# Attention loop of a two-block network: scores transposed two steps after they are made instead of one, three score buffers instead of two, and a new order of the first block's small work

## The chip, the cores and the metric

The kernel is one program on 1 core of a Trainium2 chip. The metric is device time in microseconds (us) of one execution: the median of the runs before is 1471.96 us, over 3 runs from 1471.56 to 1475.67 us.

## What is computed

The network has two blocks on 512 tokens of width 1024. Only the first block's attention is touched. It has 16 query heads of 64 columns, eight of kind A and eight of kind B. Cut to what matters:

```
o_a   = banded_gqa(qa, ka, v_a, window 128, bias, sinks)
o_cmp = softmax over 31 compressed keys            (kind B)
o_sel = softmax over the selected keys             (kind B)
o_win = banded_gqa(qb, k_win, v_win, window 512)   (kind B)
o_b   = sigmoid(g0)*o_cmp + sigmoid(g1)*o_sel + sigmoid(g2)*o_win
y     = concat(o_a * silu(z_a), o_b * silu(z_b)) @ w_out
```

With 512 tokens the 16 selected blocks of 64 cover everything, so the selected branch is full causal attention, as the window branch is.

## The kernel before, in words

**Stages.** The program runs in one stream of stages: projections of the first block, its attention, the output projection, then the second block (convolution, retention, feed-forward). Outside attention nearly all time is weight matmuls of 512 columns, each weight tile converted into a rounded high part by ACT (L444) and a low part by DVE (L449).

**The attention loop.** It is software-pipelined by hand. There are 96 steps, one for each of 4 blocks of 128 queries, 3 branches (0 is A, 1 selected, 2 window) and 8 heads. `Step` (L122) decodes the step: 8 steps make a group, 3 groups make a query block `i`. A step's width is 128 keys times its number of key blocks: one for all groups of block 0; `i + 1` in branches 1 and 2; at most two in branch 0. So steps 0 to 23 are one block wide, 24 to 55 two, 56 to 71 three, 72 to 79 two, 80 to 95 four. Every engine has its own loop over the same step number `s`, and engines meet through semaphores:

- PE (L2096): at step `s` it makes the scores of step `s` in PSUM bank 1 or 0 (two matmuls, L2112 and L2113), then the product of probabilities and values of step `s - 3` (L2129), then the transposes of the exponentials of step `s - 1` into PSUM bank 2 or 3 (issued at L2138, recorded under the helper's line L1818). The scores of `s` wait until DVE has read those of `s - 2`; a transpose waits for that step's exponential; a product waits for that step's transposed copy.
- DVE (L1424): at step `s` it adds bias and mask to the scores and takes their row minimum in one instruction (L1437, from PSUM to `sc[:, s % 2]`), after the transposes of step `s - 2` have released that buffer. Then, if `s - 1` is even, it copies the transposed exponentials of step `s - 1` from PSUM (L1451) to `pt[:, 0]`. The parts of a finished group follow two, three and four steps into the next one: reciprocal of the sums (L1467), combination with the coefficient (L1480), and for the last group an addition.
- ACT (L989): at step `s` it takes the exponential in place with the row sum (L999), and copies the transposed exponentials of `s - 1` if that is odd (L1008).
- POOL adds a finished branch into `ob` (L777) and makes remainders of rounded keys (L753).

**The tail of a query block.** `tails_at` (L144) says at which step PE transposes `oa` and `ob` of block `i` (four transposes each) and DVE multiplies them by the gates `z` (L1493); ACT rounds the result one step later (L1019), POOL makes the remainder (L764). Before: steps `24 i + 29` and `24 i + 30`, for the last block 85 and 101.

**Small work of the first block.** Before the loop DVE turns gate logits into gates (L1408, L1410) and into the compressed branch's coefficients (L1413). `compressed_out(i)` on PE (L2064) makes the compressed output of block `i` with four matmuls at steps `CO_PE_AT = (0, 2, 4, 7)`, and DVE scales it into `ob` (L1420) at `CO_AT = (1, 4, 6, 9)`. ACT rounds the window branch's keys in four pieces (`k_round(2, ...)`, L926) at `K_WINDOW_AT = (3, 4, 5, 6)`; POOL takes the remainder of each (L753), and PE waits for them at step 16. At steps 61 and 63 ACT and DVE also convert weight tiles of the next stage.

**Order.** Each engine works its queue strictly in order, so an instruction that waits holds all behind it on that engine. PE's own order at a step, in the source:

```
pe.wait_ge(m["s_bias"], s - 1)                                   # scores of s - 2 read
pe.matmul(scores, q, k_high...); pe.matmul(scores, q, k_low...)  # step s
if s in CO_PE_AT: compressed_out(...)
t = s - 3: wait pt_a / pt_d; matmuls with the values             # product
t = s - 1: wait s_exp;       transposes                          # into bank 2 + t % 2
```

Of the kernel before, what the change touches and what calls it, by code (L numbers as in the profile page):

```python
# [27 lines left out]
ACT = mybir.ActivationFunctionType  # L28
# [63 lines left out]
CONVERT_AT = 61  # L92
CO_PE_AT = (0, 2, 4, 7)
CO_AT = (1, 4, 6, 9)
K_WINDOW_AT = (3, 4, 5, 6)

# [20 lines left out]
N_ATT = 8 * N_GROUPS  # L117
STEPS = N_ATT + 9
TAIL_LAST = N_ATT + 5

# [23 lines left out]
def tails_at(s):  # L144

    return [(i, half) for i in range(NI) for half in range(2)
            if s == (24 * i + 29 + half if i < NI - 1 else 24 * i + 13 + 16 * half)]

# [35 lines left out]
def hybrid_block(nc, x, c, w_ada, b_ada, norm_gain, w_in, b_nsa_gate, q_gain_a, k_gain_a, sinks,  # L184
# [8 lines left out]
    with ExitStack() as stack:  # L193
# [97 lines left out]

        sc = sb("scores_sb", [P, 2, S], R + 24)
        pt = sb("probs_t", [P, 2, S], R + 28)
        ob = sb("out_b", [P, NI, S], R + 32)
# [92 lines left out]
        def in_slot(t, slot, half):  # L387
# [7 lines left out]
        k_low = ((proj_r[:, KC], proj_r[:, VC]), [in_slot(wlo, KS_SLOT, g) for g in range(2)],  # L395
                 [in_slot(wlo, KW_SLOT, g) for g in range(2)])

        def two(ap):
# [241 lines left out]
        def _(pool):  # L640
# [193 lines left out]
        def _(act):  # L834
# [154 lines left out]
            for s in range(STEPS):  # L989
# [3 lines left out]
                if s < N_ATT:  # L993
                    G, n = divmod(s, 8)
                    act.wait_ge(m["s_bias"], s + 1)
                    if n == 0 and G >= 2:
                        act.wait_ge(m["comb_done"], G - 1)
                    w = att(s).width
                    a.activation(sc[:, s % 2, 0:w], sc[:, s % 2, 0:w], ACT.Exp, scale=-1.0,  # L999
                                 bias=row_min[:, G % 2, n:n + 1],  # L1000
                                 accum_out=den[:, G % 2, att(s).head:att(s).head + 1]).then_inc(m["s_exp"], 1)
                t = s - 1
                if 0 <= t < N_ATT and t % 2 == 1:
# [176 lines left out]
        def _(dve):  # L1180
# [225 lines left out]
            v.tensor_copy(cpt[:, 1], ps[:, 3]).then_inc(m["cpt_ev"], 1)  # L1406
            dve.wait_ge(m["gb_done"], 1)
            own(v.tensor_scalar(gates[:], gates[:], 1.0, None, ALU.add))  # L1408
            own.wait()
            own(v.reciprocal(gates[:], gates[:]))  # L1410
            own.wait()
            for g in range(2):
                own(v.tensor_tensor(ccoef[:, :, 4 * g:4 * g + 4], cden[:, g].rearrange("p (i j) -> p i j", i=NI),  # L1413
                                    gate_of(0)[:, :, 4 * g:4 * g + 4], ALU.mult))
            own.wait()

# [7 lines left out]
            for s in range(STEPS):  # L1424
                if s < N_ATT:
                    u = att(s)
                    G = s // 8
                    dve.wait_ge(m["s_mm"], s + 1)
                    if s >= 2:
                        dve.wait_ge(m["t_mm"], s - 1)  # L1430
                    if s == 56:
                        dve.wait_ge(m["kl_done"], 11)
                    if u.branch == 0:
                        band, start = band_a[:, u.head, 256 - u.width:256], nsink[:, u.head:u.head + 1]
                    else:
                        band, start = band_b[:, u.head, S - u.width:S], 3e38
                    v.tensor_tensor_reduce(sc[:, s % 2, 0:u.width], ps[:, 1 - s % 2, 0:u.width], band, 1.0, start,  # L1437
                                           ALU.add, ALU.min, row_min[:, G % 2, s % 8:s % 8 + 1]).then_inc(m["s_bias"], 1)
                    if s % 8 == 7 and u.branch == 0:

                        dve.wait_ge(m["s_bias"], s + 1)
                        v.tensor_tensor(sink_arg[:].rearrange("p (g j) -> p j g", g=2),
                                        row_min[:, G % 2].rearrange("p (j g) -> p j g", g=2),
                                        nsink[:].rearrange("p (g j) -> p j g", g=2), ALU.subtract).then_inc(m["arg_done"], 1)
                t = s - 1
                if 0 <= t < N_ATT and t % 2 == 0:
                    dve.wait_ge(m["t_mm"], t + 1)
                    if t >= 2:
                        dve.wait_ge(m["pv_mm"], t - 1)
                    w = att(t).width  # L1450
                    v.tensor_copy(pt[:, 0, 0:w], ps[:, 2, 0:w]).then_inc(m["pt_d"], 1)  # L1451
                if s in CO_AT:
                    compressed_branch(CO_AT.index(s))
                if s in (CONVERT_AT, CONVERT_AT + 2):
                    dve_convert(dve, None, 0, U_LAST + (s - CONVERT_AT) // 2 + 1)
                G, part = divmod(s - 8, 8)
                if G >= 0 and part in (2, 3, 4):

                    i, branch = divmod(G, 3)
                    cf, dn = coef[:, G % 2], den[:, G % 2]  # L1460
                    if part == 2:
                        dve.wait_ge(m["s_exp"], 8 * G + 8)
# [6 lines left out]
                        if branch:  # L1469
                            own(v.tensor_tensor(cf, cf, gate_of(branch)[:, i], ALU.mult))  # L1470
                    elif part == 3:
                        own.wait()
# [343 lines left out]
        def _(pe):  # L1816
# [246 lines left out]

            def compressed_out(i):  # L2064

                if i == 0:
                    pe.wait_ge(m["cpt_ev"], 2)
                if i == 1:
                    pe.wait_ge(m["vt_ev"], 2)
                if i == 3:  # L2070
                    pe.wait_ge(m["co_done"], 2)
                for g in range(2):
# [23 lines left out]
            for s in range(STEPS):  # L2096
                if s < N_ATT:
# [15 lines left out]
                    pe.matmul(scores, q, k_low[u.branch][u.g][:, keys], start=False, stop=True).then_inc(m["s_mm"], 1)  # L2113
                    if s in CO_PE_AT:
                        compressed_out(CO_PE_AT.index(s))
                t = s - 3
                if 0 <= t < N_ATT:
# [13 lines left out]
                    mm.then_inc(m["pv_mm"], 1)  # L2131
                t = s - 1
                if 0 <= t < N_ATT:
# [3 lines left out]
                    for b in range(att(t).width // P):  # L2137
                        mm = trans(ps[:, 2 + t % 2, blk(b)], sc[:, t % 2, blk(b)])  # L2138
# [227 lines left out]
```

## Time and profile before

| | |
|---|---|
| median of 3 runs | 1471.96 us |
| the profiled execution's own time | 1471.78 us |
| its span, first to last instruction | 1470.1 us |
| outside the span (1471.78 - 1470.1) | 1.7 us |
| PE busy over the span | 1437.0 us (98%) |
| DVE busy | 741.1 us (50%) |
| ACT busy | 601.0 us (41%) |
| first scores of attention | 204.95 us |
| last scores of attention (step 95) | 322.19 us |

Times inside the profile count from the span's start. A row of a timeline is: start, duration, engine, line, operation, tiles, shapes, count, and in brackets how long the engine sat idle before it and what ended that. A row of a window table is: stretch, its length, then busy time of each engine with the number of instructions, the granted PE clock (1.00 is full speed), DMA share and GB/s. Durations of PE rows reach past the start of the next one, since matmuls are pipelined; the distance from one start to the next is what an instruction occupies.

### The profile page before, as it was taken

The page shows a single profiled execution, that of the slowest core. Times are in us where ns is not written, and L with a number is a line of the kernel's source. Part 1 is how long each engine was busy: PE and PEld are TensorE (multiplying, and loading weights), DVE is VectorE, ACT ScalarE, POOL GpSimd, SP SyncE. Part 2 cuts the span into 40 slices and gives each one's busy share as a digit, 9 for nine tenths or more (in the row PEclk, how much of TensorE's full clock was granted, in tenths as well). Part 3 has the DMA queues.
Part 4 walks back from the last instruction along what each step waited for, and adds up shares of the span by engine and source line. Part 5 has one row for each costly group of instructions (what it writes and reads, how often), then busy time and mean ns, then how long its engine had stood idle before and what let it go on. Part 6 is the DMA issues. An engine that isn't in the chain of part 4 may idle for free.

```text
span 1470.1 us, 18291 instructions
## 1 busy us (share of the span) xinstructions
PE 1437.0 (98%) x6990; PEld 1206.2 (82%) x6990; DVE 741.1 (50%) x1200; ACT 601.0 (41%) x1009; POOL 112.2 (8%) x131
## 2 busy tenths in 40 slices
PE   6999998999999999999999999999999999999998
PEld 5788878898888888888888888888888888888887
DVE  6741676765566533645464444454466433333332
ACT  5633566655433332333333444433355333333221
POOL 5302331110000000000000111100000000000000
PEclk9999999999999999999999999999999999999999
DMA  9995200113533333312222133343333333333321
GB/s 286 317 236 184 73 1 2 30 58 86 172 86 93 108 100 100 91 54 86 72 72 86 44 93 94 98 147 89 97 100 87 112 89 101 101 87 93 115 78 57
DMA packets 227826, 149.71 MB, mean 102 GB/s; under 512 B 5331, under 2 KB 216015, under 8 KB 227109
## 3 DMA queue, kind: packets, MB, share of 16 engines
q1 hardware_dynamic: 223588, 131.63, 30.9%
q0 software_dynamic: 4160, 17.04, 3.9%
q8 instruction: 50, 0.82, 0.2%
q14 instruction: 28, 0.22, 0.0%
HBM read 140.92 MB, written 6.68 MB: 100 GB/s over the span
## 4 chain that ended last, share of the span: by engine, by line
PE 92%; DVE 3%; issue 2%; SPq 1%; DMA 1%; ACT 1%; DVEq 0%; ACTq 0%
PE ps L429 69%; PE ps L2201 6%; PE ps L2227 3%; PE ps L1926 3%; PE ps L1818 3%; PE ps L2129 2%; PE ps L2213 1%; DMA w_raw<-in_w_in_dram 1%; PE ps L1949 1%; PE ps L1887 1%; SPq L543 1%; PE ps L1942 1%; ACT scores_sb L999 1%; DVE scores_sb L1437 1%; PE ps L2113 1%
## 5 line engine op out<-in xcount | busy, mean ns | idle before, releaser
L449 DVE TENSOR_TENSOR w_lo<-w_raw,w_hi 128x1024 fp32r<-128x1024 f32 (+1 forms) x214 | 258.1, 1209 | 251.8 <-ACT w_hi L444 249.1
L444 ACT ACTIVATE w_hi<-w_raw 128x1024 fp32r<-128x1024 f32 (+1 forms) x214 | 219.5, 1034 | 16.0 <-PE ps L429 11.3
L495 ACT ACTIVATE temps<-ps 128x512 f32<-128x512 f32 x67 | 40.0, 596 | 238.9 <-PE ps L429 238.9
L429 PE MATMUL ps<-g_hi,w_hi 128*128 128x512 f32 x384 | 95.8, 392 | 0.0
L429 PE MATMUL ps<-g_hi,w_lo 128*128 128x512 f32 x384 | 94.9, 389 | 0.0
L429 PE MATMUL ps<-g_lo,w_hi 128*128 128x512 f32 x384 | 94.8, 389 | 0.0
L429 PEld LDWEIGHTS ps<-g_hi,w_lo 128*128 128x128 f32 x384 | 72.1, 188 | 15.1
L429 PEld LDWEIGHTS ps<-g_lo,w_hi 128*128 128x128 f32 x384 | 72.1, 188 | 15.0
L429 PEld LDWEIGHTS ps<-g_hi,w_hi 128*128 128x128 f32 x384 | 71.5, 188 | 14.6
L429 PE MATMUL ps<-f_hi,w_lo 128*128 128x512 f32 x288 | 71.1, 389 | 0.0
L429 PE MATMUL ps<-f_hi,w_hi 128*128 128x512 f32 x288 | 71.1, 389 | 0.0
L429 PE MATMUL ps<-f_lo,w_hi 128*128 128x512 f32 x288 | 71.1, 389 | 0.0
L999 ACT ACTIVATE scores_sb<-scores_sb,row_min 128x256 f32<-128x256 f32 (+3 forms) x96 | 51.1, 532 | 40.1 <-DVE row_min L1437 39.4
L429 PEld LDWEIGHTS ps<-f_hi,w_lo 128*128 128x128 f32 x288 | 54.1, 188 | 11.2
L429 PEld LDWEIGHTS ps<-f_lo,w_hi 128*128 128x128 f32 x288 | 54.1, 188 | 11.2
L429 PEld LDWEIGHTS ps<-f_hi,w_hi 128*128 128x128 f32 x288 | 54.1, 188 | 11.2
L2129 PEld LDWEIGHTS ps<-proj,probs_t 128*128 128x128 f32 x432 | 58.3, 191 | 1.4
L2129 PE MATMUL ps<-proj,probs_t 128*128 128x64 f32 x432 | 59.5, 265 | 0.0
L1818 PE MATMUL ps<-ident,scores_sb 128*128 128x128 f32 x224 | 43.4, 286 | 11.2 <-ACT scores_sb L999 10.7
L429 PE MATMUL ps<-x_gain_hi,w_hi 128*128 128x512 f32 x192 | 47.8, 390 | 0.0
L429 PE MATMUL ps<-x_gain_hi,w_lo 128*128 128x512 f32 x192 | 47.6, 389 | 0.0
L429 PE MATMUL ps<-x_gain_lo,w_hi 128*128 128x512 f32 x192 | 47.6, 389 | 0.0
(436 smaller groups left out, 2691.0 us busy)
## 6 DMA issues: line engine op xcount, KB each, us to landing
w_raw<-in_w_in_dram SPq DMA_DIRECT2D x107, 512.0 KB, 3.9
w_raw<-in_w_ff_gate_dram SPq DMA_DIRECT2D x22, 512.0 KB, 3.8
w_raw<-in_w_ff_up_dram SPq DMA_DIRECT2D x22, 512.0 KB, 3.8
w_ada_shift_scale<-in_w_ada_dram SPq DMA_DIRECT2D x16, 512.0 KB, 7.8
w_raw<-in_w_r_out_dram SPq DMA_DIRECT2D x16, 512.0 KB, 4.6
w_raw<-in_w_ff_down_dram SPq DMA_DIRECT2D x16, 512.0 KB, 4.3
w_ada_gate<-in_w_ada_dram SPq DMA_DIRECT2D x4, 1024.0 KB, 10.7
x_spill<-x_t POOLq DMA_DIRECT2D x2, 2048.0 KB, 9.0
```

What stands on the lines that cost most here:

```text
L429: mm = pe.matmul(bank, w[:, slot, k], mov[:, at_k], start=first and n == 0 and k == 0, stop=last and n == 2 and k == kts - 1)
L444: act.activation(whi[:, slot, 0:kts], raw[:, slot, 0:kts], ACT.Copy).then_inc(hi_done, 1)
L449: nc.vector.tensor_tensor(wlo[:, slot, 0:kts], raw[:, slot, 0:kts], whi[:, slot, 0:kts].bitcast(F32), ALU.subtract).then_inc(lo_done, 1)
L495: act.activation(dst, ps[:, o % 4], func, scale=scale).then_inc(evac, 1)
L543: sp.dma_start(ada[:, u % 4, :, part], w_ada_v[:, :, n:n + P]).then_inc(ada_in[u % 4], 16)
L999: a.activation(sc[:, s % 2, 0:w], sc[:, s % 2, 0:w], ACT.Exp, scale=-1.0, bias=row_min[:, G % 2, n:n + 1], accum_out=den[:, G % 2, att(s). ...
L1437: v.tensor_tensor_reduce(sc[:, s % 2, 0:u.width], ps[:, 1 - s % 2, 0:u.width], band, 1.0, start, ALU.add, ALU.min, row_min[:, G % 2, s % 8 ...
L1818: return pe.transpose(dst, src, ident[0:parts, 0:parts])
L1926: mm = pe.matmul(ps[:, 4 - 4 * q + j], half_rows(w, u)[:, kk, blk(j)], h[:, 2 * c2 + kk], start=c2 == 0 and n == 0 and kk == 0, stop=c2 == ...
L2129: mm = pe.matmul(ps[:, 4 + u.group % 2, u.head * HD:(u.head + 1) * HD], pt[:, t % 2, blk(b)], proj[:, v, c:c + HD], start=b == 0, stop=b = ...
L2201: mm = pe.matmul(ps[:, 4 + j], x[:, 2 * c2 + kk, blk(j)], half_rows(w, u)[:, kk], start=c2 == 0 and n == 0 and kk == 0, stop=last and n == ...
L2227: mm = pe.matmul(ps[:, 4 + t], w[:, j, blk(t)], p[:, j], start=n == 0 and j == 0, stop=n == 2 and j == NI - 1)
```

## The change

Transposes move from step `s - 1` to `s - 2`, products from `s - 3` to `s - 4`, the transposed copies on DVE and ACT from `s - 1` to `s - 2`; the loop has one step more, and the parts of a finished group come one step later. A third buffer holds scores of every third step, and DVE's wait for its release follows. The second half of a block's tail comes at step `24 i + 32` (block 3: 102). Gates and coefficients are computed at steps 0 and 1 of the loop instead of ahead of it. The compressed output goes to PE's end of the step, for blocks 1 to 3 in two halves at two steps, and its scaling on DVE to steps 2, 6, 14, 20. The window keys are rounded at steps 4, 6, 8, 9. POOL's addition in block `i` waits for that block's compressed output alone.

```diff
-CO_PE_AT = (0, 2, 4, 7)
-CO_AT = (1, 4, 6, 9)
-K_WINDOW_AT = (3, 4, 5, 6)
+CO_PE_AT = ((0,), (2, 4), (10, 12), (16, 18))
+CO_AT = (2, 6, 14, 20)
+K_WINDOW_AT = (4, 6, 8, 9)
-STEPS = N_ATT + 9
-TAIL_LAST = N_ATT + 5
+STEPS = N_ATT + 10
+TAIL_LAST = N_ATT + 6
 def tails_at(s):
-            if s == (24 * i + 29 + half if i < NI - 1 else 24 * i + 13 + 16 * half)]
+            if s == (24 * i + 29 + 3 * half if i < NI - 1 else 24 * i + 13 + 17 * half)]
+        sc_third = sb("scores_third", [P, S], 58)
+        def sc_of(s):
+            return sc_third[:] if s % 3 == 2 else sc[:, s % 3]
 # POOL
             def add_branch(i, branch):
+                if branch == 1:
+                    pool.wait_ge(m["co_done"], i + 1)
                 if i == 0 and branch == 1:
-                    pool.wait_ge(m["co_done"], NI)
 # ACT
-                    a.activation(sc[:, s % 2, 0:w], sc[:, s % 2, 0:w], ACT.Exp, ...
+                    a.activation(sc_of(s)[:, 0:w], sc_of(s)[:, 0:w], ACT.Exp, ...
-                t = s - 1
+                t = s - 2
 # DVE: ahead of the loop -> compressed_coefficients(part), called at s < 2, after bias and copy
-            own(v.tensor_scalar(gates[:], gates[:], 1.0, None, ALU.add))
-            own(v.reciprocal(gates[:], gates[:]))
-            own(v.tensor_tensor(ccoef...
+            def compressed_coefficients(part):
+                if part:  own.wait(); (the two products into ccoef); own.wait(); return
+                dve.wait_ge(m["gb_done"], 1); (add one, reciprocal)
 # DVE: in the loop
-                    if s >= 2:
-                        dve.wait_ge(m["t_mm"], s - 1)
+                    if s >= 3:
+                        dve.wait_ge(m["t_mm"], s - 2)
-                    v.tensor_tensor_reduce(sc[:, s % 2, 0:u.width], ...
+                    v.tensor_tensor_reduce(sc_of(s)[:, 0:u.width], ...
-                t = s - 1
+                t = s - 2
+                if s < 2:
+                    compressed_coefficients(s)
-                if G >= 0 and part in (2, 3, 4):
+                if G >= 0 and part in (3, 4, 5):
 # PE
-            def compressed_out(i):
+            def compressed_out(i, groups):
-                for g in range(2):
+                for g in groups:
-                mm.then_inc(m["co_mm"], 1)
+                if 1 in groups:
+                    mm.then_inc(m["co_mm"], 1)
-                    if s in CO_PE_AT:
-                        compressed_out(CO_PE_AT.index(s))
-                t = s - 3
+                t = s - 4
-                t = s - 1
+                t = s - 2
+                for i, steps in enumerate(CO_PE_AT):
+                    if s in steps:
+                        compressed_out(i, (steps.index(s),) if len(steps) > 1 else (0, 1))
```

## Rows read from the trace of the kernel before

**Rows 1.** The page's part 1: busy time of each engine over the span.

```profile
PE 1437.0 (98%) x6990; PEld 1206.2 (82%) x6990; DVE 741.1 (50%) x1200; ACT 601.0 (41%) x1009; POOL 112.2 (8%) x131
```

**Rows 2.** Windows: steps 0-23, 24-55, 56-71, 72-79, 80-94, cut where scores start.

```profile
204.95:228.41 23.46, 18.54 (x134) 16.11 (x133) 16.03 (x75) 16.10 (x66) 10.25 (x9) 1.00 0.00 1
228.41:263.91 35.50, 31.83 (x266) 29.71 (x267) 25.33 (x96) 22.74 (x85) 6.36 (x5) 1.00 0.01 1
263.91:287.14 23.23, 21.24 (x171) 20.47 (x171) 16.98 (x52) 15.61 (x46) 3.84 (x3) 1.00 0.16 47
287.14:296.68 9.54, 9.01 (x83) 8.78 (x81) 7.08 (x24) 5.89 (x21) 1.27 (x1) 1.00 0.00 1
296.68:322.19 25.51, 25.45 (x202) 23.97 (x202) 17.85 (x49) 16.50 (x43) 5.67 (x5) 1.00 0.13 42
```

**Rows 3.** Waits from 204 to 324 us: total, times, longest one.

```profile
ACT scores_sb L999 <- DVE row_min L1437: 39.4, 45, 1.9
DVE probs_t L1451 <- PE ps L1818: 22.0, 41, 0.9
...
PE ps L1818 <- ACT scores_sb L999: 10.7, 24, 1.0
```

**Rows 4.** Timeline of PE: scores of steps 9 and 10, and of 68 and 69.

```profile
215.97 0.30 PE L2112 MATMUL ps<-w_hi,q_odd_heads 128*128 128x128 f32 x1
216.49 0.31 PE L2112 MATMUL ps<-w_hi,proj_rounded 128*128 128x128 f32 x1
...
281.54 0.42 PE L2112 MATMUL ps<-w_hi,proj_rounded 128*128 128x384 f32 x1
282.83 0.42 PE L2112 MATMUL ps<-w_hi,q_odd_heads 128*128 128x384 f32 x1
```

**Rows 5.** Timeline of all engines, two-block steps 40 to 43: one round of the loop.

```profile
246.34 0.36 PE L2112 MATMUL ps<-w_hi,proj_rounded 128*128 128x256 f32 x1
246.66 0.56 PE L2129 MATMUL ps<-proj,probs_t 128*128 128x64 f32 x4
247.05 0.39 PE L1818 MATMUL ps<-ident,scores_sb 128*128 128x128 f32 x2
247.20 0.36 PE L2112 MATMUL ps<-w_hi,q_odd_heads 128*128 128x256 f32 x1
248.07 0.44 PE L1818 MATMUL ps<-ident,scores_sb 128*128 128x128 f32 x2
248.55 0.42 DVE L1451 COPY probs_t<-ps 128x256 f32<-128x256 f32 x1 [0.40 <-PE ps L1818]
248.89 0.41 DVE L1437 CUSTOM_DVE_ANT_0 scores_sb<-ps,band_b 128x256 f32<-128x256 f32 x1
249.35 0.51 ACT L999 ACTIVATE scores_sb<-scores_sb,row_min 128x256 f32<-128x256 f32 x1 [0.56 <-DVE row_min L1437]
249.85 0.36 ACT L1008 ACTIVATE probs_t<-ps 128x256 f32<-128x256 f32 x1
250.00 0.44 PE L1818 MATMUL ps<-ident,scores_sb 128*128 128x128 f32 x2
```

**Rows 6.** Timeline of DVE: first gate instruction, and the first bias of the loop.

```profile
205.16 0.42 DVE L1408 TENSOR_SCALAR branch_gates<-branch_gates 128x96 f32<-128x96 f32 x1
...
207.09 0.35 DVE L1437 CUSTOM_DVE_ANT_0 scores_sb<-ps,band_a,sinks_negated 128x128 f32<-128x128 f32 x1
```

**Rows 7.** Timeline: POOL's last remainders of window keys; PE's scores of step 16.

```profile
215.39 2.68 POOL L753 TENSOR_TENSOR w_lo<-proj,w_hi 64x512 fp32r<-64x512 f32 x2 [1.24 <-ACT w_hi L926]
...
222.03 0.30 PE L2112 MATMUL ps<-w_hi,proj_rounded 128*128 128x128 f32 x1
```

**Rows 8.** Windows: the start of the span, where the granted clock is below 1.00.

```profile
15.00:20.00 5.00, 1.01 (x4) 0.93 (x4) 4.96 (x13) 2.29 (x7) 5.00 (x11) 0.80 1.16 312
20.00:25.00 5.00, 4.17 (x10) 3.33 (x11) 4.97 (x11) 2.77 (x5) 5.00 (x11) 0.52 1.16 304
```

More of the change, by code:

```diff
@@ L998, in _ @@
                     w = att(s).width
-                    a.activation(sc[:, s % 2, 0:w], sc[:, s % 2, 0:w], ACT.Exp, scale=-1.0,
+                    a.activation(sc_of(s)[:, 0:w], sc_of(s)[:, 0:w], ACT.Exp, scale=-1.0,
                                  bias=row_min[:, G % 2, n:n + 1],
                                  accum_out=den[:, G % 2, att(s).head:att(s).head + 1]).then_inc(m["s_exp"], 1)
-                t = s - 1
+                t = s - 2
                 if 0 <= t < N_ATT and t % 2 == 1:
@@ L1406, in _ @@
             v.tensor_copy(cpt[:, 1], ps[:, 3]).then_inc(m["cpt_ev"], 1)
-            dve.wait_ge(m["gb_done"], 1)
-            own(v.tensor_scalar(gates[:], gates[:], 1.0, None, ALU.add))
-            own.wait()
-            own(v.reciprocal(gates[:], gates[:]))
-            own.wait()
-            for g in range(2):
-                own(v.tensor_tensor(ccoef[:, :, 4 * g:4 * g + 4], cden[:, g].rearrange("p (i j) -> p i j", i=NI),
-                                    gate_of(0)[:, :, 4 * g:4 * g + 4], ALU.mult))
-            own.wait()
+            def compressed_coefficients(part):
+                if part:
+                    own.wait()
+                    for g in range(2):
+                        own(v.tensor_tensor(ccoef[:, :, 4 * g:4 * g + 4], cden[:, g].rearrange("p (i j) -> p i j", i=NI),
+                                            gate_of(0)[:, :, 4 * g:4 * g + 4], ALU.mult))
+                    own.wait()
+                    return
+                dve.wait_ge(m["gb_done"], 1)
+                own(v.tensor_scalar(gates[:], gates[:], 1.0, None, ALU.add))
+                own.wait()
+                own(v.reciprocal(gates[:], gates[:]))
             def compressed_branch(i):
@@ L1436, in _ @@
                         band, start = band_b[:, u.head, S - u.width:S], 3e38
-                    v.tensor_tensor_reduce(sc[:, s % 2, 0:u.width], ps[:, 1 - s % 2, 0:u.width], band, 1.0, start,
+                    v.tensor_tensor_reduce(sc_of(s)[:, 0:u.width], ps[:, 1 - s % 2, 0:u.width], band, 1.0, start,
                                            ALU.add, ALU.min, row_min[:, G % 2, s % 8:s % 8 + 1]).then_inc(m["s_bias"], 1)
@@ L1456, in _ @@
                 G, part = divmod(s - 8, 8)
-                if G >= 0 and part in (2, 3, 4):
+                if G >= 0 and part in (3, 4, 5):
                     i, branch = divmod(G, 3)
                     cf, dn = coef[:, G % 2], den[:, G % 2]
-                    if part == 2:
+                    if part == 3:
                         dve.wait_ge(m["s_exp"], 8 * G + 8)
@@ L1470, in _ @@
                             own(v.tensor_tensor(cf, cf, gate_of(branch)[:, i], ALU.mult))
-                    elif part == 3:
+                    elif part == 4:
                         own.wait()
@@ L2071, in compressed_out @@
                     pe.wait_ge(m["co_done"], 2)
-                for g in range(2):
+                for g in groups:
                     mm = pe.matmul(ps[:, CO_BANK[i], 256 * g:256 * g + 256], cpt[:, g, blk(i)], vbd[:, g], start=True, stop=True)
-                mm.then_inc(m["co_mm"], 1)
+                if 1 in groups:
+                    mm.then_inc(m["co_mm"], 1)
             def out_unit(tokens, parts):
@@ L2137, in _ @@
                     for b in range(att(t).width // P):
-                        mm = trans(ps[:, 2 + t % 2, blk(b)], sc[:, t % 2, blk(b)])
+                        mm = trans(ps[:, 2 + t % 2, blk(b)], sc_of(t)[:, blk(b)])
                     mm.then_inc(m["t_mm"], 1)
+                for i, steps in enumerate(CO_PE_AT):
+                    if s in steps:
+                        compressed_out(i, (steps.index(s),) if len(steps) > 1 else (0, 1))
                 if s == TAIL_LAST:
```

## The prediction

> **What bounds the kernel now.** I read the page's busy times first, then windows cut where the scores of the stages start, then the waits of attention, then single steps in the timeline. PE is busy 98% of the span [rows 1], so whatever PE does not wait for now can give little. The windows show where it does wait: in the 117.2 us from the first to the last scores of attention PE is idle 4.92 us in the one-block steps, 3.67 in the two-block steps 24 to 55, 1.99 in the three-block steps, 0.53 in steps 72 to 79 and 0.06 in the four-block steps [rows 2], 11.2 us together. The reader is to see that the idle share falls as the steps get wider. DVE and ACT are busy only 16.0 and 16.1 of the first 23.46 us [rows 2], so no engine is full there: a dependency is what ends last.
>
> The waits name it. PE's transposes wait 10.7 us for exponentials, ACT's exponentials 39.4 us for DVE's biases, DVE's copies 22.0 us for PE's transposes [rows 3]. These three form a ring, and rows 5 show one round of it: transposes of step 40 start at 248.07, DVE's copy of them at 248.55 (0.48 later), behind it in DVE's queue the bias of step 42 at 248.89 (0.34), the exponential of 42 at 249.35 (0.46), the transposes of 42 at 250.00 (0.65). That is 1.93 us for two steps, 0.965 a step. PE by itself needs less: scores of 40 and of 41 start 0.86 apart where PE did not wait [rows 5]. In one-block steps that distance is 0.52, in three-block steps 1.29 [rows 4].
>
> **The change, part by part.** *Depth and third buffer.* The transposes of 42 now come a step later, so the ring above is cut. The next one goes from the transposes of 40 (step 42) to DVE's copy (0.48), the bias of 43 (0.34), its exponential (0.46), ACT's copy of 41 behind it (0.50) and that copy's own 0.36 and about 0.1 to reach PE, then the product of 41 in step 45, from which PE goes to the transposes of 44 in step 46: 0.39 within a step (246.66 to 247.05) and one more step of 0.86 [rows 5]. The sum is 3.49 us for four steps, 0.87 a step, practically PE's own 0.86. I take 0.88, because the sink branch's bias has more to do. For the 32 steps from 24 to 55 that is 32 x (0.965 - 0.88) = 2.7 us. The buffer itself costs nothing: DVE's wait for its release names the transposes of `s - 3`, which PE issues ahead of the scores that the same bias needs. Two score banks and two copies stay.
>
> *Tails three steps apart.* Two gate products no longer fall into neighbouring steps of DVE. What rows 2 leave after PE's own pace is 35.50 - 32 x 0.86 = 8.0 us, of which the sixteen transposes of four tails take some 1.6 (estimated at 0.1 each, from two within the 0.15 to 0.2 us ahead of 247.20 [rows 5]). Of 6.4 us the ring gives 2.7; of the other 3.7, combinations and tails, I credit a quarter, 0.9, since a combination still holds DVE once in each group. Two-block steps together: 3.6 us, between 0 and 6.4.
>
> *Three-block steps.* 23.23 - 16 x 1.29 = 2.6 us over PE's pace, 1.99 idle [rows 2, 4]. The two weight conversions in DVE's and ACT's queues stay, so I take 1.5, between 0 and 2.6. *Steps 72 to 79:* the idle 0.53 [rows 2], taken whole at 0.5. *Four-block steps:* PE waits for nothing [rows 2], 0.
>
> *Gates and coefficients inside the loop.* They stand between 205.16 and 207.09 ahead of the first bias [rows 6], while the first scores were issued at 204.95 [rows 2]. The first bias can start some 1.9 us earlier; the same 1.9 us now stand behind the biases of steps 0 and 1, and what is queued there is the biases of 1 and 2, for which the scores of 3 and 4 wait. With PE not yet transposing, I count 1.9 as won, 0 as the other end. *Compressed output and window keys.* The matmuls and scalings are as many as before, spread until step 20, where a scaling meets a combination in DVE's queue; I credit nothing and charge nothing. ACT's last key rounding moves from step 6 to 9. POOL's remainders ended at 215.39 + 2.68 = 218.07 and step 16 was at 222.03 [rows 7]; even with step 9 at its old 215.97 [rows 4], the rounding would have to end after 222.03 - 1.34 = 220.7 to hold PE. Nothing. POOL's addition waits for less than before. Of the remaining 4.92 - 1.9 = 3.0 us of idle in these 24 steps I take a quarter, 0.8, as the three engines' loads lie close (16.0, 16.1 and PE's 18.5 [rows 2]) and one's delay has no room to be absorbed. Block 0 together: 2.7, between 0 and 4.9.
>
> *The end of the loop.* One step more: the transposes and product of one four-block step move behind the last scores. The stage lasts 25.51 / 15 = 1.7 us a step [rows 2], so at most 1.7 could be exposed; it is work moved from ahead of those scores, so I charge 0. SP's queue has no edit in it; the reload of the residual on POOL follows the step count and shifts along.
>
> **Sum:** 2.7 + 3.6 + 1.5 + 0.5 = 8.3 us. The profiled execution took 1471.78 us (span 1470.1 and 1.7 around it), 0.2 under the median, so 1463.5 us.
>
> The ceiling is a choice of gauge. By PE's idle time it is 11.2 us. By step starts it is higher, since two- and three-block steps have 2.7 and 0.6 us more over PE's pace than they show idle: 14.5. The Trainium skill (Perfetto Trace Analysis, Identifying the Most-Contended Engine) calls matmul busy time a poor measure of how far PE is from its limit, as matmuls are pipelined, and prefers the share of weight loads. Here weight loads fill 23.97 of 25.51 us in the stage that does not wait and 75.07 of 91.73 before it [rows 2]; at the same 94% those 75.07 would fit in 79.9, a ceiling of 11.8. The trace agrees with it in direction only, and the sum stands without it.
>
> **Rivals.** *All of it.* The queues settle and PE is never held: 11.2 to 14.5 us, 1457.3 to 1460.6. For it: in the four-block steps DVE and ACT keep ahead at the old depth [rows 2]. Against it: each combination sits between two biases as before, and the new ring has 0.01 us of room in two-block steps. Chance 0.16.
>
> *The copies become the ring.* Only two transposed copies and two PSUM banks for transposes remain, and ACT's copy stands behind a later exponential. If DVE's wait for the transposes comes back in this place, two-block steps stay at 0.965. For it: the 3.49 us above hold no slack, so 0.4 us more of queueing in each four steps restores the old pace. Left are 1.9 at the start, 0.5 in steps 72 to 79 and half of the 1.99 in three-block steps: 3.4 us, 1468.4. Chance 0.20, a little over half of it within 0.3%.
>
> *Slower: the clock.* PE's granted clock is 1.00, its 2.4 GHz level, in all of attention [rows 2]. At the start of the span it fell to 0.80 in five microseconds in which PE was busy 1.01, and to 0.52, nearly the 1.2 GHz level, in the next five [rows 8]. If the reordered first steps left PE idle like that, the 18.5 us of PE work of block 0 would take up to twice as long: 1463.5 + 18.5 = 1482.0. It decides once more than 8.3 us of work run at half speed. Against it: 18.54 of 23.46 us busy kept the clock at 1.00, and the change asks PE to wait less. Chance 0.04.
>
> *Nothing happens.* DVE's order keeps everything where it was, 1471.8. DVE's copies in step 42 no longer stand ahead of that step's bias, so this would need another chain of the same length. Chance 0.02.
>
> **The numbers.** The forecast has the remaining 0.58. A change of 0.3%, 4.4 us, is about what a measurement of this kernel can tell from none, so faster means under 1467.5: the forecast, all of it, and 0.09 of the copies' ring, 0.83; same 0.13; slower 0.04. The range goes from the lowest bound, 1457.0, to 1468.0, where the copies' ring is centred.
>
> **What would show it.** Step starts of two-block scores at 0.87 to 0.89 us rather than 0.965; PE's wait on exponentials at L1818 down from 10.7 to under 3 us, DVE's wait on transposes down from 22.0; first bias near 205.3, last scores near 314; four-block steps unchanged at 1.7. I would be wrong if waits reappear at the products (L2129, on DVE's or ACT's copies) with two-block steps still at 0.96, if step 16 waits for POOL, or if the granted clock is below 1.00 between 205 and 330 us.

## The result, and the profile after

The changed kernel takes 1461.41 us (median of 4 runs, 1460.96 to 1461.91), the kernel before 1473.59 us beside it (4 runs, 1471.56 to 1475.67): a ratio of 0.9912, 95% interval 0.9899 to 0.9924. The forecast was 1463.5 us, the range 1457.0 to 1468.0. The profiled executions give the mechanism: 1471.78 us before and 1461.91 after, 9.9 us less. The executions of the kernel before lie in two groups by their mean granted TensorE clock, so its median lies between 1471.96 and 1474.53 us in the sets of runs here; the forecast was made against one of the upper group (0.997), and the last section tells more.

The page's busy times after, as [rows 1] before:

```profile
PE 1436.3 (98%) x6990; PEld 1207.1 (83%) x6990; DVE 741.5 (51%) x1200; ACT 601.3 (41%) x1009; POOL 112.4 (8%) x131
```

The work is the same; only waiting went. The windows of the five stages after, cut where the scores of steps 0, 24, 56, 72, 80 and 95 start, as [rows 2] before:

```profile
204.94:224.99 20.05, 17.69 (x131) 15.49 (x130) 15.30 (x75) 15.42 (x65) 10.17 (x9) 1.00 0.01 1
224.99:256.74 31.75, 30.92 (x262) 29.70 (x260) 24.91 (x95) 23.29 (x85) 6.50 (x6) 0.95 0.01 2
256.74:277.57 20.83, 20.67 (x173) 19.95 (x172) 18.15 (x52) 15.44 (x46) 3.84 (x3) 1.00 0.19 52
277.57:286.27 8.70, 8.67 (x81) 8.46 (x80) 6.56 (x23) 6.03 (x21) 1.28 (x1) 1.00 0.01 3
286.27:311.06 24.79, 24.79 (x202) 23.56 (x200) 18.26 (x48) 16.90 (x44) 5.68 (x5) 1.00 0.13 44
```

The stages are shorter by 3.41, 3.75, 2.40, 0.84 and 0.72 us, 11.1 together. The span is shorter by 9.9: 1.2 us come back behind the last scores, where one four-block step's transposes and product now stand. In steps 56 to 71 PE's idle time falls from 1.99 to 0.16 us, in steps 24 to 55 from 3.67 to 0.83 (there the granted clock was 0.95; e1 below, at 1.00, shows 1.05). The waits of attention after, 204 to 313 us, to be read beside [rows 3]:

```profile
ACT scores_sb L1004 <- DVE row_min L1447: 21.4, 33, 1.7
...
ACT scores_third L1004 <- DVE row_min L1447: 6.8, 13, 1.1
DVE probs_t L1461 <- PE ps L1830: 6.3, 17, 0.6
...
PEld ps L2140 <- ACT probs_t L1013: 5.5, 16, 0.6
```

And PE's own waits, 195 to 330 us:

```profile
PE ps L2140 <- ACT probs_t L1013: 2.3, 8, 0.4
...
PE ps L1830 <- ACT scores_sb L1004: 0.2, 1, 0.2
```

All three edges of the old ring shrank: PE on exponentials 10.7 to 0.2, ACT on biases 39.4 to 28.2 over both kinds of buffer, DVE on transposes 22.0 to 6.3. A new wait is there: the product waits for ACT's transposed copy, L1013. The timeline of all engines around step 40 of the changed kernel shows how:

```profile
238.80 0.68 DVE L1492 TENSOR_TENSOR out_a<-ps,coefficient 128x512 f32<-128x512 f32 x1
238.94 0.39 PE L1830 MATMUL ps<-ident,scores_third 128*128 128x128 f32 x2
...
239.40 0.41 DVE L1447 CUSTOM_DVE_ANT_0 scores_sb<-ps,band_b 128x256 f32<-128x256 f32 x1
...
239.86 0.51 ACT L1004 ACTIVATE scores_sb<-scores_sb,row_min 128x256 f32<-128x256 f32 x1 [0.85 <-DVE row_min L1447]
...
240.36 0.36 ACT L1013 ACTIVATE probs_t<-ps 128x256 f32<-128x256 f32 x1
...
240.78 0.66 PE L2140 MATMUL ps<-proj,probs_t 128*128 128x64 f32 x4 [0.35 <-ACT probs_t L1013]
...
241.42 0.36 PE L2125 MATMUL ps<-w_hi,proj_rounded 128*128 128x256 f32 x1
```

A combination holds DVE, the bias is late behind it, the exponential waits 0.85 us for the bias, and ACT's copy at 240.36, whose input PE had transposed at 238.94, stands behind that exponential. Step 40 starts 1.48 us after step 39 (239.94). The next three starts are 242.28, 243.13 and 243.99: 0.86 apart, PE's own pace.

### The profile page after: what moved, and what is told of

The parts are those of the page before. It is cut to its first block, busy times and chain, and to the rows that moved or that the text cites. A ratio compares the mean times of both kernels' runs of the same rounds, so it can differ in the third digit from the quotient of the medians.

```text
span 1460.2 us, 18290 instructions
## 1 busy us (share of the span) xinstructions
PE 1436.3 (98%) x6990; PEld 1207.1 (83%) x6990; DVE 741.5 (51%) x1200; ACT 601.3 (41%) x1009; POOL 112.4 (8%) x131
## 4 chain that ended last, share of the span: by engine, by line
PE 95%; SPq 1%; DMA 1%; DVE 1%; ACT 1%; issue 1%; DVEq 0%; ACTq 0%
PE ps L433 70%; PE ps L2215 6%; PE ps L2241 3%; PE ps L1938 3%; PE ps L2140 3%; PE ps L1830 3%; PE ps L2227 1%; DMA w_raw<-in_w_in_dram 1%; PE ps L1961 1%; PE ps L1899 1%; PE ps L2126 1%; PE ps L2125 1%; SPq L547 1%; PE ps L1954 1%; SPq L577 0%
## 5 line engine op out<-in xcount | busy, mean ns | idle before, releaser
L1798 DVE TENSOR_TENSOR temps<-temps 128x512 f32<-128x512 f32 x22 | 15.2, 691 | 59.1 <-ACT temps L499 58.8
L433 PE MATMUL ps<-act_hi,w_hi 128*128 128x512 f32 x176 | 43.8, 389 | 0.0
```

The lines of the kernel that those rows point to most:

```text
L433: mm = pe.matmul(bank, w[:, slot, k], mov[:, at_k], start=first and n == 0 and k == 0, stop=last and n == 2 and k == kts - 1)
L1798: v.tensor_tensor(tt[:, 4], tt[:, t % 2], tt[:, 2 + t % 2], ALU.mult).then_inc(m["prod_done"], 1)
```

## The experiments

Lengths of the stages, in us, from windows cut as above, each beside the median of its runs. A star marks a stage with a granted clock under 1.00. The changed kernel and the experiments ran in sets (the change; e1 to e4; e5 to e8; e9 to e12). The kernel before had medians of 1473.59, 1473.64, 1474.53 and 1474.40 us beside them, so a difference of less than 1 us between kernels of different sets tells nothing.

| kernel | 0-23 | 24-55 | 56-71 | 72-79 | 80-94 | median |
|---|---|---|---|---|---|---|
| before | 23.46 | 35.50 | 23.23 | 9.54 | 25.51 | 1473.59 |
| after | 20.05 | 31.75* | 20.83 | 8.70 | 24.79 | 1461.41 |
| e1 depth only | 20.13 | 30.72 | 20.85 | 8.70 | 24.78 | 1461.42 |
| e2 order only | 22.59 | 35.51 | 23.23 | 9.53 | 25.51 | 1471.52 |
| e3 two buffers | 27.00* | 39.60* | 23.86 | 10.88 | 26.83 | 1483.63 |
| e4 tails adjacent | 20.01 | 31.41 | 20.37 | 9.13 | 24.53 | 1461.23 |
| e5 copy first | 19.39 | 28.66 | 20.11 | 8.38 | 24.78 | 1457.84 |
| e6 scaling apart | 19.39 | 30.71 | 20.83 | 8.68 | 24.79 | 1460.33 |
| e7 both | 18.80 | 28.64 | 20.09 | 8.39 | 24.78 | 1456.79 |
| e8 gates in loop | 24.20* | 36.14* | 23.23 | 9.53 | 25.52 | 1472.71 |
| e9 two buffers, copy first | 20.81 | 32.78* | 20.63 | 8.68 | 25.43 | 1464.28 |
| e10 copies later | 27.43* | 42.22* | 26.60 | 11.49 | 30.46 | 1494.26 |
| e11 copies later, first | 22.04 | 34.83 | 22.23 | 9.42 | 26.47 | 1469.49 |
| e12 depth, copy first | 19.14 | 28.66 | 20.11 | 8.38 | 24.78 | 1456.99 |

**e1, depth without the new order of the first block** (main lines of the edit).

```diff
-CO_PE_AT = ((0,), (2, 4), (10, 12), (16, 18)); CO_AT = (2, 6, 14, 20); K_WINDOW_AT = (4, 6, 8, 9)
+CO_PE_AT = (0, 2, 4, 7); CO_AT = (1, 4, 6, 9); K_WINDOW_AT = (3, 4, 5, 6)
-                if s < 2: compressed_coefficients(s)      # gates ahead of the loop again
```

> The changed kernel with its first-block order undone: gates and coefficients ahead of the loop, compressed output and key rounding at their old steps. Theory (cutting the ring of transposes, copy, bias and exponential gives what is won from step 24 on): two-block steps run at 0.86 to 0.88 us, last scores come 8 to 9.5 us earlier than the 322.19 us of the kernel before, and the time is 1463.5 to 1466, because block 0 wins 0 to 2 us instead of 3.4. Rival (the new order of the small work does most of it): 1469 to 1471.

Ratio 0.9915 (0.9898 to 0.9931), 1461.42 us: the whole gain, and below both forecasts, since block 0 won more than the 0 to 2 us allowed for. Windows of steps 0-23 and 24-55:

```profile
205.66:225.79 20.13, 17.70 (x132) 15.59 (x130) 16.21 (x75) 15.66 (x65) 10.22 (x9) 1.00 0.00 1
225.79:256.51 30.72, 29.67 (x261) 28.25 (x260) 24.84 (x95) 23.21 (x85) 6.51 (x6) 1.00 0.01 2
```

Depth, third buffer and tails alone win 3.33 us in the first block and 4.78 in the two-block steps.

**e2, the new order without the depth**: the kernel before, with the gates, the compressed output, the key rounding and POOL's addition as in the change (main lines of the edit).

```diff
-CO_PE_AT = (0, 2, 4, 7); CO_AT = (1, 4, 6, 9); K_WINDOW_AT = (3, 4, 5, 6)
+CO_PE_AT = ((0,), (2, 4), (10, 12), (16, 18)); CO_AT = (2, 6, 14, 20); K_WINDOW_AT = (4, 6, 8, 9)
+                if s < 2: compressed_coefficients(s)
```

> The kernel before with the new order of the first block's small work alone, depth and two score buffers as they were. Theory: one-block steps win 1.9 to 3.4 us, two-block steps stay at 0.965 us a step and win nothing, time 1468.5 to 1470. Rival (order does most): below 1466.

Ratio 0.9991 (0.9982 to 1.0001), 1471.52 us: no change that can be told, and above both forecasts. The first block is 0.87 us shorter (22.59), and no other stage moves. Where the head start goes is seen in the starts of the scores, counted from the first score of each kernel:

| scores of step | 2 | 8 | 14 | 20 | 24 |
|---|---|---|---|---|---|
| before | 3.17 | 9.89 | 15.62 | 19.97 | 23.46 |
| e2 order only | 1.98 | 7.55 | 14.05 | 19.10 | 22.59 |
| e1 depth only | 2.57 | 8.35 | 12.84 | 17.19 | 20.13 |
| after | 1.93 | 6.63 | 12.06 | 16.52 | 20.05 |

The order puts step 8 2.3 us ahead at the old depth and 1.7 at the new one. From there to step 24, where half of the compressed output now stands (steps 10 to 18 in place of 4 and 7, its scalings at 14 and 20 in place of 6 and 9), nearly all of it is lost: 0.87 and 0.08 are left. Part of the head start is thus work put off. e8, where the compressed output keeps its old steps, is 1.33 us ahead of the kernel before at step 8 and still 1.29 at step 14.

**e3, the change with two score buffers.**

```diff
-            return sc_third[:] if s % 3 == 2 else sc[:, s % 3]
+            return sc[:, s % 2]
-                    if s >= 3: dve.wait_ge(m["t_mm"], s - 2)
+                    if s >= 2: dve.wait_ge(m["t_mm"], s - 1)
```

> The changed kernel with two score buffers instead of three, so that the bias of a step waits for the transposes of two steps before, which PE issues behind that step's scores. Theory (the depth is what counts; transposes to bias 0.48, bias to exponential 0.46, exponential to transposes 0.65 are 1.6 us in two steps, less than PE's 1.72): two-block steps stay near 0.86 to 0.90, one-block steps rise to about 0.67, time 1462 to 1465. Rival (the third buffer is what gives the gain): two-block steps back at 0.96, time 1467 to 1471.

Ratio 1.006 (1.004 to 1.008), 1483.63 us: 22 us over the changed kernel, slower than before and outside both forecasts. The clock fell in some of its executions, but the two at 0.996 took 1480.8 and 1481.94 us too. Two two-block steps take 2.42 us (scores at 253.06 and 255.48). The timeline of all engines over such a pair:

```profile
252.91 0.39 PE L1830 MATMUL ps<-ident,scores_sb 128*128 128x128 f32 x2
...
253.45 0.42 DVE L1447 CUSTOM_DVE_ANT_0 scores_sb<-ps,band_b 128x256 f32<-128x256 f32 x1 [0.80 <-PE ps L1830]
...
253.92 0.51 ACT L1004 ACTIVATE scores_sb<-scores_sb,row_min 128x256 f32<-128x256 f32 x1 [0.96 <-DVE row_min L1447]
...
254.42 0.36 ACT L1013 ACTIVATE probs_t<-ps 128x256 f32<-128x256 f32 x1
...
254.84 0.66 PE L2140 MATMUL ps<-proj,probs_t 128*128 128x64 f32 x4 [0.40 <-ACT probs_t L1013]
...
255.34 0.39 PE L1830 MATMUL ps<-ident,scores_sb 128*128 128x128 f32 x2
```

The bias can't start before the transposes of two steps earlier, and each link follows the one before it: 0.54 + 0.47 + 0.50 + 0.42 + 0.50 = 2.43. The prediction's "the buffer itself costs nothing" stands, but the depth without it is a loss.

**e4, the tails in neighbouring steps.**

```diff
-            if s == (24 * i + 29 + 3 * half if ...
+            if s == (24 * i + 30 + half if ...
```

> The changed kernel with the two halves of a block's tail one step apart again (steps 24 i + 30 and 24 i + 31). Theory: the prediction credited 0.9 us to spreading them in the two-block steps, so 0.6 to 1.5 us slower than the changed kernel, 1462 to 1463. Rival (the deeper loop absorbs them wherever they stand): within 0.3 us of the changed kernel, 1461.1 to 1461.7.

1461.23 us, ratio 0.9915 (0.9898 to 0.9932). Steps 24-55 take 0.69 us more than in e1 and 72-79 0.43 more, steps 56-71 0.48 and 80-94 0.25 less: the tails move between the stages, and their spacing is worth nothing that can be measured, as the rival said.

**e5, ACT's copy ahead of the exponential.**

```diff
 # ACT, step s
+                t = s - 2: wait t_mm; a.activation(pt[:, 1, 0:w], ps[:, 3, 0:w], ACT.Copy)
                 if s < N_ATT: wait s_bias; a.activation(sc_of(s)..., ACT.Exp)
-                t = s - 2: wait t_mm; a.activation(pt[:, 1, 0:w], ps[:, 3, 0:w], ACT.Copy)
```

> The changed kernel with one edit: ACT copies the transposed exponentials of step s - 2 ahead of the exponential of step s, not behind it. Theory A: what is left of PE's idle time in two- and three-block steps is the chain bias behind a combination, exponential, ACT's copy queued behind that exponential, product. The copy is ready to run earlier (its transposes are a step old), so the products' waits on ACT's copies (5.5 + 2.3 us in the changed kernel) fall below 3 us, steps 24 to 55 fall from 31.75 to 30.0 to 30.7 us, and the whole is 1458.5 to 1460.5 us. Theory B: the copy put first holds up the exponential by 0.36 to 0.5 us, or waits itself for the transposes, and the transposes wait in place of the products; the waits move and the time is 1461 to 1463 us.

1457.84 us (1457.53 to 1458.44), ratio 0.9889 (0.9872 to 0.9905), 3.6 us under the changed kernel: theory A, and more than it said. The same swap alone lies between e6 and e7, which ran in one set: 3.5 us. Windows of steps 24-55 and 56-71, then PE's waits on copies, 204 to 315 us:

```profile
225.63:254.29 28.66, 28.44 (x260) 27.82 (x260) 25.36 (x97) 23.12 (x84) 6.91 (x6) 1.00 0.01 2
254.29:274.40 20.11, 20.11 (x174) 20.04 (x172) 18.13 (x53) 15.63 (x46) 3.85 (x3) 1.00 0.19 54
```

```profile
PEld ps L2140 <- ACT probs_t L1004: 0.6, 2, 0.4
...
PE ps L2140 <- ACT probs_t L1004: 0.3, 1, 0.3
```

The products' waits on ACT fall from 5.5 and 2.3 to 0.6 and 0.3, and PE is busy 28.44 of 28.66 us. The wait after step 39 was one of many of its kind. Beside e1, whose clock is 1.00 in that stage too, steps 24 to 55 are 2.06 us shorter.

**e6, the last scaling at step 22.** In the changed kernel it meets a combination on DVE at step 20. DVE's timeline there, and the scores of PE that waited for the bias:

```profile
222.45 0.68 DVE L1430 TENSOR_TENSOR out_b<-ps,compressed_coefficient 128x512 f32<-128x512 f32 x1
223.05 0.68 DVE L1492 TENSOR_TENSOR out_tmp<-ps,coefficient 128x512 f32<-128x512 f32 x1
223.65 0.28 DVE L1447 CUSTOM_DVE_ANT_0 scores_sb<-ps,band_b 128x128 f32<-128x128 f32 x1
...
223.99 0.33 PE L2125 MATMUL ps<-w_hi,q_odd_heads 128*128 128x128 f32 x1 [0.49 <-DVE row_min L1447]
```

```diff
-CO_AT = (2, 6, 14, 20)
+CO_AT = (2, 6, 14, 22)
```

> The changed kernel with one edit: the last scaling of the compressed output on DVE at step 22 in place of 20, so that it no longer meets a combination in the same step. Theory A: the meeting fills DVE at 222 to 224 us, PE idles half a microsecond, and the granted clock falls to 0.50 at 226 to 228; with the meeting gone the clock stays at 1.00 and steps 24 to 55 take 30.7 us as in the kernel with depth alone, the whole 1460.2 to 1460.7 us. Theory B: the dip doesn't hang on this meeting (it is there in one execution and not in the next); the clock may be either, and the median stays at 1461.0 to 1461.8 us.

1460.33 us (1459.94 to 1460.58), 1.1 under the changed kernel: within theory A's bounds. The first block is 0.66 us shorter, and the clock is 1.00 in all stages. But the meeting alone doesn't bring the fall of the clock: e4 has the same meeting and kept 1.00 (rows in the last section).

**e7, both edits.**

> The changed kernel with both edits: ACT's copy ahead of the exponential, and the last scaling at step 22. Theory A of each holds: 1457.5 to 1460 us, faster than either alone. Theory B of each: 1461 to 1463 us, as the changed kernel.

1456.79 us (1456.42 to 1457.74), ratio 0.9884 (0.9868 to 0.9901): about what the two edits give one by one, 1.1 under e5 and below theory A's range. No run is faster; e12 is not told apart from it.

**e8, the kernel before with the gates alone in the loop** (main lines of the edit).

```diff
-CO_AT = (1, 4, 6, 9)
+CO_AT = (2, 4, 6, 9)
-            own(v.tensor_scalar(gates...)); own(v.reciprocal(gates...)); own(v.tensor_tensor(ccoef...))
+                if s < 2: compressed_coefficients(s)
```

> The kernel before (one stage less of depth, two score buffers) with the gates and coefficients alone moved into steps 0 and 1, and the first scaling at step 2. The prediction's step: the first bias starts 1.9 us earlier and 1.9 us are won in steps 0 to 23, 23.46 to 21.6 us, 1471.8 to 1469.9 us on the profiled execution. Rival: what stood ahead of the first bias now stands behind it, and the ring of the old depth sets the pace of steps 2 to 23; 0 to 0.9 us are won there (22.6 to 23.5 us), as with the whole new order of the first block, and the time is 1471 to 1472 us.

1472.71 us, ratio 0.9988 (0.9978 to 0.9997): above both forecasts and nearer the rival's. The first bias did start early (205.39), but step 2 starts 2.00 us after the first score, 1.2 ahead of the kernel before, and step 14 14.33 us after it, 1.3 ahead: not 1.9. PE's timeline of the kernel before, then of e8, shows why:

```profile
208.04 0.33 PE L1818 MATMUL ps<-ident,scores_sb 128*128 128x128 f32 x1 [0.99 <-ACT scores_sb L999]
```

```profile
205.37 1.13 PE L2079 MATMUL ps<-v_compressed_diagonal,compressed_probs_t 128*128 128x256 f32 x4
...
206.70 0.30 PE L2118 MATMUL ps<-proj_rounded,q_odd_heads 128*128 128x128 f32 x1
...
206.95 0.30 PE L1824 MATMUL ps<-ident,scores_sb 128*128 128x128 f32 x1
```

In the kernel before, PE idled only 0.99 us for the first exponential. In both kernels the scores of step 1 start 1.7 us after those of step 0, behind the first compressed output, and the first transposes come after them, however early the bias is. Then the clock fell in this execution, so its first block (24.20) can't be read for the rest; the rows stand in the last section.

**e9, two score buffers with the copy first** (e3's and e5's edits together).

> The changed kernel with two score buffers, as in e3, and ACT's copy ahead of the exponential. Theory A: what cost 22 us in e3 was one chain, bias waiting for the transposes of s - 2, exponential, ACT's copy behind that exponential, product, transposes (2.42 us for two steps). With the copy first the chain ends at the exponential; what is left is transposes, bias (0.54), DVE's copy behind it (0.34), its 0.42 and 0.1 to reach PE, product to transposes (0.39): 1.79 us for two two-block steps, 0.90 a step, little over PE's 0.86. Steps 24 to 55 take 29 to 31 us, and the time is 1459 to 1466 us. Theory B: the third buffer is needed at this depth whatever the order, since the bias waits for transposes that PE issues a step later than before: the time stays above 1473 us.

1464.28 us, ratio 0.9931 (0.9915 to 0.9948): theory A in the time, 19 us under e3 by the order of two instructions on ACT (17 under e3's two executions at 0.996). Steps 24-55 took 32.78 us, over theory A's 31, with the clock at 0.95. Against e5, the same kernel with three buffers, the third is then still worth 6.4 us.

**e10, the kernel before with both copies a step later.**

```diff
 # ACT and DVE, transposed copies
-                t = s - 1
+                t = s - 2
```

> The kernel before with one edit: both transposed copies a step later in their queues (s - 2), transposes (s - 1), products (s - 3) and the two score buffers as before. DVE's copy no longer stands ahead of the bias, so the prediction's old ring is cut. Theory A: what counts is where the copies stand. ACT's copy now stands behind the exponential of s, and the product of s - 2 follows in the next step: transposes, bias (0.54), exponential (0.46), copy (0.51 behind it, 0.36 long, 0.1 to reach PE), product to transposes (0.39): 2.36 us for two steps, as e3's 2.42. Steps 24 to 55 take 37 to 40 us and the time is 1478 to 1486 us, slower than before. Theory B: the old ring was all that held PE, and cutting it is enough: 1461 to 1468 us.

Ratio 1.0141 (1.0124 to 1.0158), 1494.26 us: slower as theory A said, by more than it said. Its sum was for two-block steps alone, but the three- and four-block steps are longer than before too, by 3.37 and 4.95 us with the clock at 1.00; in the first two stages the clock was 0.75 and 0.96 and takes a part that no run separates. Timeline of one pair of two-block steps:

```profile
252.16 0.66 PE L2129 MATMUL ps<-proj,probs_t 128*128 128x64 f32 x4 [0.57 <-ACT probs_t L1008]
...
252.80 0.36 PE L2112 MATMUL ps<-w_hi,q_odd_heads 128*128 128x256 f32 x1
...
253.32 0.42 DVE L1437 CUSTOM_DVE_ANT_0 scores_sb<-ps,band_b 128x256 f32<-128x256 f32 x1 [0.93 <-PE ps L2113]
...
253.79 0.51 ACT L999 ACTIVATE scores_sb<-scores_sb,row_min 128x256 f32<-128x256 f32 x1 [1.10 <-DVE row_min L1437]
...
254.30 0.36 ACT L1008 ACTIVATE probs_t<-ps 128x256 f32<-128x256 f32 x1
...
254.71 0.66 PE L2129 MATMUL ps<-proj,probs_t 128*128 128x64 f32 x4 [0.57 <-ACT probs_t L1008]
```

The pair takes 254.71 - 252.16 = 2.55 us, on e3's chain but for its start: the product now stands ahead of the scores, and the bias waits for them (0.52 after 252.80) and not for the buffer. The old ring is cut and a longer one has taken its place.

**e11, e10 with ACT's copy first.**

> As e10, and ACT's copy ahead of the exponential. Theory A: with both rings cut, neither the added depth nor the third buffer is needed: the longest chain is the one by DVE's copy, 1.79 us for two two-block steps, 0.90 a step; steps 24 to 55 take 29 to 31.5 us and the time is 1459 to 1467 us. Theory B: the added depth and the third buffer themselves bring the gain: two-block steps stay at 0.96, steps 24 to 55 above 34 us, and the time is above 1469 us.

1469.49 us, ratio 0.9969 (0.9956 to 0.9981): 25 us under e10, but outside theory A's 1459 to 1467. (One of its seven executions took 5599.5 us, for a reason that no run shows; the other six took 1469.4 to 1470.07.) Its timeline over a pair of two-block steps names what is left:

```profile
244.16 0.66 PE L2129 MATMUL ps<-proj,probs_t 128*128 128x64 f32 x4
...
244.80 0.36 PE L2112 MATMUL ps<-w_hi,proj_rounded 128*128 128x256 f32 x1
...
245.32 0.42 DVE L1437 CUSTOM_DVE_ANT_0 scores_sb<-ps,band_b 128x256 f32<-128x256 f32 x1 [0.70 <-PE ps L2113]
...
245.67 0.42 DVE L1451 COPY probs_t<-ps 128x256 f32<-128x256 f32 x1
...
246.15 0.66 PE L2129 MATMUL ps<-proj,probs_t 128*128 128x64 f32 x4
```

1.99 us for two steps, now by DVE's copy behind the bias of scores that PE had only just made. Theory A counted this chain from the transposes to the transposes (1.79) and left out that DVE's bias waits for the scores behind them. So theory B is right here: depth, third buffer and the tails' spacing bring the rest, e11 to e12 12.5 us.

**e12, depth and copy first, in the old order of the first block** (e1's and e5's edits together).

> Depth and third buffer as in the change, ACT's copy ahead of the exponential, and the first block's small work in the order of the kernel before (gates ahead of the loop, compressed output, scaling and key rounding at the old steps). Theory A: the new order adds nothing, here either: steps 0 to 23 take 18.8 to 19.5 us as in e5 and e7, the time is 1456.5 to 1458.5 us. Theory B: with PE nearly full the order counts: steps 0 to 23 take 20 us or more, and the time is 1459 to 1460.5 us.

1456.99 us (1456.34 to 1457.49), ratio 0.9885 (0.9868 to 0.9901): theory A. The first block takes 19.14 us, against e5's 19.39 and e7's 18.80: with the copy first, too, the new order wins nothing that can be told.

## Why the prediction was right, and where its terms were not

*The mechanism.* Right: PE lost its time to the ring of transposes, DVE's copy, bias and exponential, and the depth cut it. Two-block steps run at 0.86 where nothing else happens (0.87 to 0.89 expected), the first bias is at 205.31 (205.3), PE's wait on exponentials is 0.2 (under 3), and the last scores start at 311.06 (314). One of the prediction's own signs of being wrong did come: the granted clock is below 1.00 between 205 and 330 us, 0.50 from 226 to 228. It cost about 1 us of the changed kernel's profiled execution (31.75 us in steps 24 to 55, e1 30.72).

*The ring's term was too small.* "32 x (0.965 - 0.88) = 2.7 us" and a quarter of the rest of block 0's idle time, 0.8, were measured by e1 at 4.78 and 3.33 us. Of the two-block steps' 4.78 the ring itself is 32 x (0.965 - 0.86) = 3.4; what was mis-sized is the pace (0.88 for 0.86) and the share of the stalls around combinations that would stay. The four longest of these steps, 2.17, 1.66, 1.67 and 2.17 us before, take 1.30, 1.48, 1.52 and 1.29 in e1. Three-block steps gave 2.40 for 1.5, steps 72 to 79 0.84 for 0.5.

*Gates and coefficients, "I count 1.9 as won".* Wrong. At the old depth the whole order wins 0.87 us in block 0, on top of the depth 0.08. Two steps failed. The first bias did start 1.8 us earlier, but PE could take only 1.2 to 1.3 of it, since its own work stood ahead of the scores of step 1 (e8). And for the neighbour, the compressed output, "I credit nothing and charge nothing": in the change the early start is given back in the steps into which that work was moved. At the new depth, 0.66 us of it is shown to be the scaling that meets a combination (e6); for the other 1.0 the place, and e8's steady lead without the move, are all that speak.

*Tails, 0.9.* Nothing (e4).

*Two terms too high and four too low* made 8.3 of a measured 9.9 us. That the sum was nearer than its parts is luck.

*Four-block steps, 0, and the drain, 0.* The stage is 0.72 us shorter though PE waited for nothing in it. It is moved work: the starts of steps 80 and 86 lie 9.12 us apart after, 9.83 before, since narrower transposes and products now stand in steps 80 to 83; from step 86 on both go 1.74 to 1.75 a step. The 1.2 us behind the last scores give it back; the other 0.5 is not traced.

*The rivals.* "The copies become the ring" named the right place and the wrong price: the wait at the products is the new one (5.5 and 2.3 us), but it is not met in every step: of PE's eight such waits five fall into the one-block steps, and the three from step 24 on come some 2 us behind a combination (238.80, 246.40, 263.72). It cost 3.6 us (e5), where the rival charged the old pace. With two buffers, e3, the copy does become the ring, at 1.21 us a two-block step. "All of it" went to at most 14.5 us by PE's step starts; e7's profiled execution takes 1456.42 us, 15.4 less than before, so even that was no ceiling. The 94% of weight loads was none either: in e5's steps 56 to 71 they fill 20.04 of 20.11 us. The slower rival, the clock: a fall did come, but behind the first block, and for some 3 us. That the new order brings it is not shown, since e4 has the order and no fall.

*What stays open.* How the gain splits between depth and third buffer. With the copy first, the third buffer is worth 6.4 us (e9 to e5), depth without it 5.2 (e11 to e9, which differ in the first block's order and the tails too, and e9 has a clock dip). Three buffers at the old depth were not tried. What the gates' new place is worth apart from the rest is known only from e8.

## What to carry to other kernels

In a loop pipelined by hand over in-order engines, look at what an instruction whose input is old stands behind: put it ahead of the one whose input is new. The same two instructions of ACT, swapped, were worth 3.6 us with three buffers, 17 to 19 with two and up to 25 at the old depth, where a part is the clock. A stage of depth needs its buffer with it (e3 lost some 20 us without), and work that is spread over later steps is paid there, so count it where it lands and not only where it leaves.

## What was not expected of the hardware

PE's granted clock falls during attention, in some executions and not in others. Windows of the changed kernel, 222 to 230 us, behind the meeting on DVE shown at e6:

```profile
222.00:224.00 2.00, 1.45 (x13) 1.11 (x12) 2.00 (x9) 0.83 (x6) 0.19 (x1) 1.00 0.02 4
224.00:226.00 2.00, 1.75 (x11) 1.61 (x11) 0.85 (x6) 1.65 (x8) 1.08 (x1) 0.75 0.00 0
226.00:228.00 2.00, 2.00 (x12) 2.00 (x12) 1.36 (x6) 1.31 (x5) 0.00 (x0) 0.50 0.00 0
228.00:230.00 2.00, 2.00 (x19) 2.00 (x17) 1.71 (x9) 1.32 (x6) 0.00 (x0) 0.90 0.00 0
```

And of e8, the kernel before with the gates in the loop:

```profile
217.00:220.00 3.00, 2.23 (x14) 1.96 (x15) 1.94 (x10) 1.81 (x10) 2.03 (x2) 0.81 0.03 5
220.00:223.00 3.00, 3.00 (x18) 3.00 (x18) 1.27 (x9) 1.80 (x8) 0.00 (x0) 0.50 0.00 0
...
232.00:235.00 3.00, 2.96 (x26) 2.83 (x25) 2.59 (x10) 1.50 (x7) 0.00 (x0) 0.91 0.01 3
```

PE idles a little, then the clock goes to 0.50, the 1.2 GHz level, while PE is busy, and comes back after some 3 us in the one and 14 in the other. The share of idle time alone doesn't tell when. The profiled execution of the kernel before was busy 2.80 of the 4 us from 217 to 221 and kept 1.00, and so did e4's, which has the order of the changed kernel and was busy for the same 1.45 and 1.75 us:

```profile
222.00:224.00 2.00, 1.45 (x11) 1.17 (x10) 1.97 (x8) 0.83 (x6) 0.57 (x1) 1.00 0.00 0
224.00:226.00 2.00, 1.75 (x16) 1.70 (x16) 1.17 (x6) 1.52 (x8) 0.71 (x1) 1.00 0.00 0
```

The Trainium skill (TensorE: Matmul & The Clock Gate, A second HAM failure mode: psum-queue depth-cycling) describes a PE whose clock swings between two levels as it pauses briefly and often between groups of matmuls. The traces agree in the two levels and in the pauses ahead of each fall, but the two above show one fall and one return each, and e4's the pauses without a fall.

The price is seen in the executions. Of 36 of the kernel before, run beside the experiments, 9 had a mean granted clock of 0.997 and took 1471.68 to 1472.6 us, and 27 had 0.990 to 0.994 and took 1473.64 to 1476.53. The 28 of the changed kernel, e1, e4 to e7 and e12 all had 0.995 to 0.997, and 9 of e2's 10. So the change wins 10.5 us against executions at 0.997 (median 1471.89; 9.9 between the two traces), and 1.8 to 4.6 more where the kernel before has the lower mean. By the same reading, e8's four executions at 0.996 or 0.997 took 1470.65 to 1472.11 us (median 1471.17): 0.7 us for the gates alone, which is its rival's size. The only trace of the kernel before is at 0.997; that the others lose their clock in attention, as e8 does, is likely and not shown.
